# Expert rows of a two-part transformer kernel: first-table rows of both token tiles ahead of second-table rows, other shares of rows per stage, and the second layer's modulation moved to the first block's scores

## The reference, cut to what matters

```python
for l in range(DEPTH):
    mod   = (silu(c)     @ w_mod[l] + b_mod[l])     # six rows of 1024: shift, scale, gate, twice
    mod_c = (silu(c_ctx) @ w_mod[l] + b_mod[l])     # the same for the context
    ...                                              # mixer: attention, pooling, convolution, gates, w_out
    xn2 = modulate(rms_norm(h, norm2_g[l]), mod[:, 3], mod[:, 4])
    h = h + mod[:, 5] * peer_ffn(xn2, ...)           # and for the context where not last

def peer_ffn(x, w_q, sub_keys, u_emb, v_emb):        # per chunk of 128 tokens
    q = (xc @ w_q) ...                               # 8 heads, two halves of 128
    ... top 16 of each half's 128 keys, top 16 of the 256 sums -> eidx, gate = softmax
    u = u_emb[eidx]                                  # 128 rows of 1024 for each token
    hid = gelu(einsum('td,thkd->thk', xc, u))
    return einsum('thk,thkd->td', gate * hid, v_emb[eidx])
```

## Time and profile before

| | |
|---|---|
| median of 3 runs | 3910.57 us (3910.49 to 3939.74) |
| the profiled execution | 3915.19 us, span of its instructions 3913.4 us |
| DVE busy | 2804.7 us (72%) |
| PE busy | 1916.9 us (49%), weight loads 1225.8 us |
| POOL busy | 1842.7 us (47%) |
| ACT busy | 402.6 us (10%) |
| DMA | 1111.66 MB, mean 284 GB/s; gathers 811.71 MB of it |

### The profile page before, as it was taken

How to read it: one execution, slowest core, us unless ns; L and a number is a source line. 1 busy time by engine, 2 the same in 40 slices (tenths; PEclk the granted TensorE clock), 3 DMA queues, 4 the chain that set the end, 5 groups by cost and what they waited for, 6 DMA issues and landing times.

```text
span 3913.4 us, 27165 instructions
## 1 busy us (share of the span) xinstructions
PE 1916.9 (49%) x8842; PEld 1225.8 (31%) x8842; DVE 2804.7 (72%) x4787; ACT 402.6 (10%) x917; POOL 1842.7 (47%) x1556
## 2 busy tenths in 40 slices
PE   6899993076885698883206000019899800000000
PEld 3558482044532346463202000004475700000000
DVE  2321279945869987759997999975411699998998
ACT  1310110023211310010001000002300100000000
POOL 0000033423636766627746777740000377577776
PEclk8999997588786699996557555559999955555555
DMA  6754487767889899969969999963144588699999
GB/s 206 248 178 166 161 289 254 222 232 258 293 313 349 302 355 372 391 243 402 392 232 358 372 380 396 374 249 140 66 149 167 198 291 283 235 377 361 386 377 345
DMA packets 402292, 1111.66 MB, mean 284 GB/s; under 512 B 37121, under 2 KB 91585, under 8 KB 401378
## 3 DMA queue, kind: packets, MB, share of 16 engines
q0 software_dynamic: 223024, 811.71, 56.2%
q1 hardware_dynamic: 179128, 298.22, 21.6%
HBM read 1105.52 MB, written 4.29 MB: 284 GB/s over the span
## 4 chain that ended last, share of the span: by engine, by line
DVE 36%; PE 33%; POOL 13%; DMA 8%; issue 8%; ACT 2%; DVEq 0%; SPq 0%; ACTq 0%; POOLq 0%
PE PS L419 30%; POOL ring L975 13%; DVE acc L1332 12%; DVE ring L1326 11%; DMA ring<-in_peer_u,eidx 3%; DMA wring<-in_w_in 2%; DVE work L1774 1%; DVE work L1777 1%; DVE work L1386 1%; DVE work L1775 1%; ACT work L1002 1%; DMA ring<-in_peer_v,eidx 1%; DVE work L1389 1%; DVE work L1833 1%; DVE work L1836 1%
## 5 line engine op out<-in xcount | busy, mean ns | idle before, releaser
L975 POOL DMA_INDIRECT ring<-in_peer_u,eidx x768 | 940.2, 1224 | 1297.8 <-DVE eidx L1839 515.7
L975 POOL DMA_INDIRECT ring<-in_peer_v,eidx x768 | 892.4, 1162 | 615.4 <-DVE acc L1332 219.6
L1332 DVE SCALAR_TENSOR_TENSOR acc<-ring,small,acc 128x1024 f32<-128x1024 f32 x762 | 977.4, 1283 | 90.9 <-DMA ring<-in_peer_v,eidx 27.9
L1326 DVE SCALAR_TENSOR_TENSOR ring<-ring,xn_peer 128x1024 f32<-128x1024 f32 x768 | 932.9, 1218 | 77.6 <-DMA ring<-in_peer_u,eidx 67.5
L419 PE MATMUL PS<-wring,xnT 128*128 128x512 f32 (+2 forms) x1728 | 738.9, 589 | 17.8 <-issue 13.1
L419 PE MATMUL PS<-xnT,wring 128*128 128x128 f32 (+1 forms) x2896 | 484.1, 330 | 28.1 <-DMA wring<-in_w_in 17.2
L419 PEld LDWEIGHTS PS<-xnT,wring 128*128 128x128 f32 x2896 | 440.6, 195 | 70.9 <-DMA wring<-in_w_in 19.6
L419 PEld LDWEIGHTS PS<-wring,xnT 128*128 128x128 f32 x1728 | 330.2, 194 | 418.9 <-issue 411.2
L427 PE MATMUL PS<-const,work 128*128 128x128 f32 (+1 forms) x358 | 59.2, 331 | 696.8 <-DVE work L1389 676.8
L1002 ACT ACTIVATE work<-PS 128x512 f32<-128x512 f32 (+5 forms) x377 | 189.2, 525 | 1133.7 <-PE PS L419 771.8
L419 PE MATMUL PS<-wring,work 128*128 128x512 f32 (+2 forms) x640 | 265.1, 576 | 29.1 <-DMA wring<-in_w_out 17.3
(11 more groups left out here) (163 smaller groups left out, 1486.0 us busy)
## 6 DMA issues: line engine op xcount, KB each, us to landing
wring<-in_w_in SPq DMA_DIRECT2D x128, 1024.0 KB, 7.4
wring<-in_w_mod SPq DMA_DIRECT2D x48, 1024.0 KB, 12.9
wring<-in_peer_wq SPq DMA_DIRECT2D x24, 1024.0 KB, 7.3
wring<-in_ab_w_in SPq DMA_DIRECT2D x13, 1024.0 KB, 21.9
wring<-in_conv_out_w SPq DMA_DIRECT2D x12, 1024.0 KB, 5.1
wring<-in_w_out SPq DMA_DIRECT2D x12, 1024.0 KB, 9.3
ring<-in_peer_u,eidx POOLq DMA_INDIRECT x768, 6.4
ring<-in_peer_v,eidx POOLq DMA_INDIRECT x768, 6.1
```

The costliest lines, as they stand in the source:

```text
L975: pool.indirect_dma_start(ring[:, m % NG, :], None, table, bass.IndirectOffsetOnAxis(ap=eidx[:, r % 2, t, k:k + 1], axis=0))\
L1326: v.scalar_tensor_tensor(out=slot, in0=slot, scalar=1.0, in1=xn_peer[:, t, :], op0=ALU.mult, op1=ALU.mult, accum_out=hid[:, k:k + 1]).then ...
L1332: v.scalar_tensor_tensor(out=acc[:, :], in0=slot, scalar=wgt[:, k - NSEL:k - NSEL + 1], in1=acc[:, :], op0=ALU.mult, op1=ALU.add).then_inc ...
```

## The change

The order of items within a run becomes: first-table rows of tile 0, of tile 1, then second-table rows and gate row of tile 0, of tile 1. For that, `hid` and `wgt` get a copy for each tile. Tile 0 of run 0 is turned at "ab", ahead of the first scores, and tile 1 at "gated c", between the z gates and y of the latent attention. `PACE` and `PER_PRODUCT` are lower in "ab" and "c"; in mixer 1 the pace is lower and the number per product goes from 5 to 8. In `gelu_first` fewer rows than before may be left; four rows are done between it and `gelu_last` in runs 1 and 2.

The second layer's modulation moves from behind run 1's queries to the place between `vb` and the first scores: on PE, on ACT (ahead of `top_exps(0)`), in SP's order of weights (ahead of the z weights of ab_in). Its bias comes in one DMA of 12 rows instead of three, into a space that is free there; the matmul that adds it takes a column of the identity and 12 rows instead of ones and one row. `mod_out` for it stands before block ("ab_in", 9), and DVE waits for `mod_stored` before it first writes `O_TOK`, which shares its space.

```diff
-PACE = {"front0": 0.3, "ab": 0.8, "c": 0.8, "m1": 0.7, "front1": 0.5, "m3": 0.8, "front2": 0.5}
-PER_PRODUCT = {"ab": 6, "c": 6, "m1": 5, "m3": 4}
+PACE = {"front0": 0.3, "ab": 0.5, "c": 0.5, "m1": 0.5, "front1": 0.5, "m3": 0.8, "front2": 0.5}
+PER_PRODUCT = {"ab": 4, "c": 4, "m1": 8, "m3": 4}
-TURN_AT = {"c": (0, 0), "pooled 1": (0, 1)}
+TURN_AT = {"ab": (0, 0), "gated c": (0, 1)}
 # weight_blocks
-    halves("ab_in", "ab_w_in", 0, 7 * WB, 3328, 7)
+    halves("ab_in", "ab_w_in", 0, 7 * WB, 9 * WB, 7)
+    halves("mod1_0", "w_mod", 1, 0, 2 * D)
+    halves("mod1_1", "w_mod", 1, 2 * D, 6 * D)
+    halves("ab_in", "ab_w_in", 0, 9 * WB, 3328, 9)
...
-    halves("mod1_0", "w_mod", 1, 0, 2 * D)
-    halves("mod1_1", "w_mod", 1, 2 * D, 6 * D)
 # items
+        RUN_ITEMS = T * (2 * NSEL + 1)
+        def u_item(r, t, k):
+            return RUN_NO[r] * RUN_ITEMS + t * NSEL + k
+        def v_item(r, t, k):
+            return RUN_NO[r] * RUN_ITEMS + T * NSEL + t * (NSEL + 1) + k
 # PE, modulation
-                    pe.wait_ge(modb_landed, 48 * (l + 1))
+                    pe.wait_ge(modb_landed, 16 * (l + 1))
...
-                        ins = pe.matmul(strips[j], const[0:1, C_ONES:C_POOL], MODROW[l][m // 4][0:1, at_b:at_b + P], start=False, stop=True)
+                        ins = pe.matmul(strips[j], this, MODB[l][:, j * P:(j + 1) * P], start=False, stop=True)
 # PE, first_block
                 tokens("ab_in", 2, xnT, ("vb",), 7)
+                modulation(1, 0)
+                modulation(1, 1)
 # SP
-                    sp.wait_ge(*at("product", "wo", 1, T - 1, 1))
-                for n in range(3):
-                    sp.dma_start(MODROW[l][n][0:1, :], ...).then_inc(modb_landed, 16)
+                    sp.wait_ge(*at("product", "sub", 0, T - 1, GROUPS - 1))
+                sp.dma_start(MODB[l], DR["b_mod_2"][l].rearrange("(m c) -> m c", m=12)).then_inc(modb_landed, 16)
...
-                ("ab_in", 9): [(load_bias, 2), (load_bias, 3)],
+                ("ab_in", 9): [(mod_out, 1, 0, 3), (load_bias, 2), (load_bias, 3)],
-                ("k3", 0): [(mod_out, 1, 0, 3), (load_rows, "sc_3", "sh_3"), (load_smalls, 1)],
+                ("k3", 0): [(load_rows, "sc_3", "sh_3"), (load_smalls, 1)],
 # POOL
             for r in range(3):
                 for t in range(T):
+                    rows_in(r, t, DR["peer_u_2"].rearrange("l e d -> (l e) d"), u_item)
+                for t in range(T):
+                    rows_in(r, t, DR["peer_v_2"].rearrange("l e d -> (l e) d"), v_item)
 # ACT, first_block
                 same("act", "vb_ready")
+                modulation(1, 0)
+                modulation(1, 1)
                 top_exps(0)
+                turn("ab")
 # DVE
-                    if m >= min(rows_at["chosen"], rows_at["weighted"] * NI + NSEL):
+                    if m >= rows_at["chosen"] if u_row else r * T + t >= rows_at["weighted"]:
                         return
...
+                        if s == "ab" and u == 2:
+                            v.wait_ge(mod_stored, 128)
...
+                turn_to_v("ab")
                 pace("ab")
...
-            expert_rows(2 * NI * T)
             gelu_first(1, 0)
+            expert_rows(4)
             gelu_last(1, 0)
             pace("m3")
             mixer(3, [("product", "xnT", ("m", 1), T - 1, 1)])
-            expert_rows(NI * T)
             gelu_first(1, 1)
+            expert_rows(4)
             gelu_last(1, 1)
-            expert_rows(NI * T)
+            expert_rows(RUN_ITEMS)
...
             for t in range(T):
-                expert_rows(NI * T)
                 gelu_first(2, t)
+                expert_rows(4)
                 gelu_last(2, t)
-            expert_rows(NI * T)
+            expert_rows(RUN_ITEMS)
```

More of the change, by code:

```diff
@@ L290, in program @@
         early = ring[:, :, :].rearrange("p n d -> p (n d)")
-        MODROW = [[early[0:2, b:b + 2 * D] for b in (0, 2048, 4096)], [work[0:2, b:b + 2 * D] for b in (0, 2048, 4096)]]
+        MODB = [early[0:12, 0:512], work[0:12, 11776:12288]]
         mod_rows = xn_peer[:, :, :].rearrange("p t d -> p (t d)")
         MODT = [[mod_rows[:, 512 * a:512 * b].rearrange("p (a b) -> p a b", b=P) for a, b in ((0, 1), (1, 3))],
-                [wk(6144, 4, P), wk(6656, 8, P)]]
+                [wk(10240, 4, P), wk(10752, 8, P)]]
         hot = early[0:33, 6144:7168].rearrange("p (g j) -> p g j", g=2)
@@ L965, in _, with rows_in @@
             pool.wait_ge(mod_stored, 64)
-            def rows_in(r, t, table, kinds):
+            def rows_in(r, t, table, item):
                 for k in range(NSEL):
-                    m = item(r, t, kinds * NSEL + k)
-                    if not kinds and k % (NSEL // GROUPS) == 0:
+                    m = item(r, t, k)
+                    if item is u_item and k % (NSEL // GROUPS) == 0:
                         pool.wait_ge(*at("experts", r, t, k // (NSEL // GROUPS)))
@@ L1013, in gelu_exp @@
                 act.wait_ge(*at("gelu_arg", r, t))
-                A(act.activation(wgt, wgt, ACT.Exp, scale=-1.0), "gelu_exp", r, t)
+                A(act.activation(wgt[:, t, :], wgt[:, t, :], ACT.Exp, scale=-1.0), "gelu_exp", r, t)
             def root(dst, src, waits, *tag):
@@ L1294, in _ @@
             peer_front(1)
-            modulation(1, 0)
-            modulation(1, 1)
             top_exps(1)
@@ L1317, in expert_rows @@
                     m = rows_at["next"]
[L1318 removed]
+                    r, j = m // RUN_ITEMS, m % RUN_ITEMS
+                    u_row = j < T * NSEL
+                    t, k = (j // NSEL, j % NSEL) if u_row else ((j - T * NSEL) // (NSEL + 1), (j - T * NSEL) % (NSEL + 1))
+                    if m >= rows_at["chosen"] if u_row else r * T + t >= rows_at["weighted"]:
                         return
                     rows_at["next"] += 1
[L1321 removed]
                     slot = ring[:, m % NG, :]
                     v.wait_ge(g_landed[m % NG], 16 * (m // NG + 1))
[L1324 removed]
+                    if u_row:
                         v.scalar_tensor_tensor(out=slot, in0=slot, scalar=1.0, in1=xn_peer[:, t, :], op0=ALU.mult,
[L1327 to L1330 removed]
+                                               op1=ALU.mult, accum_out=hid[:, t, k:k + 1]).then_inc(slot_used, 1)
+                    elif k == 0:
+                        v.tensor_scalar(acc[:, :], slot, wgt[:, t, 0:1], None, ALU.mult).then_inc(slot_used, 1)
+                    elif k < NSEL:
                         v.wait_ge(slot_used, m)
[L1332 removed]
+                        v.scalar_tensor_tensor(out=acc[:, :], in0=slot, scalar=wgt[:, t, k:k + 1], in1=acc[:, :],
                                                op0=ALU.mult, op1=ALU.add).then_inc(slot_used, 1)
@@ L1783, in mixed_norm @@
                 v.wait_ge(*row_wait(f"m2_{r}"))
+                assert rows_at["next"] >= (v_item(r - 1, 0, 0) if r else 0)
                 for t in range(T):
@@ L1839, in choose @@
                 D_(v.tensor_copy(eidx[:, r % 2, t, at_n], placef[:, 0, at_n]), "experts", r, t, g)
-                rows_at["chosen"] = job * NI + n * (g + 1) if g < GROUPS - 1 else (job + 1) * NI
+                rows_at["chosen"] = u_item(r, t, n * (g + 1))
             def peer_front(r, free, beside_first=None):
```

47 lines of the change are left out of this document (17 added, 30 removed).

## The result

The changed kernel takes 3944.66 us (median of 20 runs, 3933.88 to 3953.37), the kernel before on the same chip 3918.55 (20 runs, 3901.42 to 3947.79): **1.0059** times as long [1.0045, 1.0074] (a ratio over all runs; the quotient of the two medians is 1.0067). The forecast was 13 us less than before, in a range up to 3938; measured is some 0.3 to 0.6% more. The profiled span went from 3913.4 to 3944.1, so 30.7 us have to be found.

What follows compares the result with a forecast made beforehand. The prediction took VectorE (DVE), nearly always busy with gathered rows, as the bound. Its stage terms summed to -13 us, giving 3902 us for an execution like the profiled one and 3898 for the median, range 3855 to 3938.

Steps and rivals of the forecast that it cites:

- the flush at the gates of "c": Latent attention's gates: 38 rows at 1.32 = 50 us; with GELU, ten rows and additions 71 against 35 now, +36.
- "ab", with the modulation beside front0: First attention: flush of 30 rows 40 us, GELU 3.8, 8 fewer rows -10, modulation beside front0 3; together +37.
- "c" up to the gates: Latent attention before its gates: 10, 11 and 6 fewer rows give -20 us, -12 if the chain holds.
- mixer 1: heads, attention, behind it: Mixer 1: ten more rows in the heads +4 us, 67 rows become 48 in the attention -17, behind it -3.
- front1: Choosing of run 1: -12 and -12 us, then two full blocks of 42.5 and 5 closing rows +35; together +11.
- run 3's keys, rows before mixer 2: 5 more rows beside run 3's keys and values +3 us; before mixer 2, 68 first-table rows out, 29 second-table in, -50.
- front2: Choosing of run 2: two full choose blocks and 5 rows more, +35 us.
- the end: Last stretch of rows alone: 34 first-table rows fewer at 1.44 us each, -49 us.
- The modulation: Second modulation beside front0: matmuls free, weights in near 742, no DVE wait near 762; 3 us charged there, 12 returned in front1.
- (1): Rival: bytes decide in mixer 1, chains do not bind; part behind its attention gains 24 us, total 3859; chance 0.28.
- (2): Rival: modulation weights end at 791, so DVE stalls 29 us at 762; total 3927; chance 0.09.
- (3): Rival: crowded rows cost +20 us in mixer 1, +9 at the gates of "c", whose chain gives only 12; 3938; chance 0.08.

Runs made afterwards that it cites:

- m1_rates_old: Changed kernel with mixer 1's rates as before (0.7 and 5), those of "ab" and "c" as changed; ratio 1.0034 to the kernel before.
- after_again: The changed kernel unchanged, measured a second time with the kernel before beside it; ratio 1.0029.
- mod_back: Changed kernel with the second modulation put back behind run 1's queries; ratio 1.0057 to the kernel before.
- first_rates_old: Changed kernel with the rates of "ab" and "c" as before (0.8 and 6), mixer 1's as changed; ratio 0.9927 to the kernel before.
- turn_late: Changed kernel, its rates kept, with tile 1 of run 0 turned at mixer 1's pooling instead of "gated c"; ratio 0.9955 to the kernel before.
- ab_rates_old: Changed kernel with the rates of "ab" alone as before (0.8 and 6); ratio 0.9944 to the kernel before.
- c_rates_old: Changed kernel with the rates of "c" alone as before (0.8 and 6); ratio 0.9992 to the kernel before.
- ab_more: Changed kernel with all rates as before, except 10 instead of 6 rows per product in "ab"; ratio 0.9980 to the kernel before.
- before_again: The kernel before, unchanged, profiled once more; one run, 3921.45 us.
- mod_only: Kernel before with the second modulation alone moved, old order and old rates; ratio 0.9965 to the kernel before.
- fronts_07: Changed kernel with all rates as before, and pace 0.7 in place of 0.5 in front1 and front2; ratio 0.9946 to the kernel before.

## Why the prediction was wrong

The sign was wrong, and the range missed by 7 us. Of the 47 us between 3898 and 3944.66, 8 are not the change's: the kernel before has 3910.57 in its three runs and 3918.55 in twenty. The counts and the places where things wait were forecast rightly. What failed is what rows cost in the places they were moved to, and most of all one term of the sum, the flush at the gates of "c". In the forecast's terms, with the closing steps of front1 and front2 counted to them as there:

| step | forecast | measured |
|---|---|---|
| "ab", with the modulation beside front0 | +37 | +39 |
| "c" up to the gates, and flush with y | -20, +36 | -14, +48 |
| mixer 1: heads, attention, behind it | +4, -17, -3 | +13, -18, 0 |
| front1 | +11 | +13 |
| run 3's keys, rows before mixer 2 | +3, -50 | +3, -43 |
| mixer 2 | 0 | +2 |
| front2 | +35 | +33 |
| the end | -49 | -45 |

The sum of the right column is +31, of the left one -13.

- **The flush at the gates, the step that failed most.** It was priced "38 rows at 1.32 = 50", the price of a row that has the DMA engines to itself. It took 62.5 us, 1.64 a row (62 to 63 us in all four traces that have it), because the weights of the coming products come at just that place (a third of the engines' time) and PE has nothing to do beside it once y is done at 1121. The forecast named this ("c_out's weights and the next ones want the DMA engines, too") and gave it at most 9 us, and the rival that the crowding costs 9. The flush in "ab" took 45.5 us for 30 rows, 1.52 each, not 40; no weights came beside that one (from 764 to 811 the DMA share was 0.87, all of it gathers), so its price has another reason, which stays open.
- **"c" up to the gates.** 27 rows fewer give 14 us, 0.5 each, as by the chain's bound (-12), not 20.
- **The heads.** +13, not +4. The ten further rows were thought to be half hidden behind the wait for q. But the last two places of 8, 16 rows in 22.1 us, stand between the operands and the first score's reduction. In m1_rates_old, with 9 rows fewer there, the heads take 144.9 us for after_again's 156.9: 1.33 a row, nothing hidden.
- **Rows alone.** The -90 for 68 first-table rows held. But "a row alone costs another price in the new order", named as what would make the forecast wrong, happened: the 60 that remain, items 710 to 769, took 92.4 us from first start to last, 1.57 each, where the same rows took 1.29 before (+16). They now lie directly behind run 3's keys, where the last weights for mixer 2 still come; the first 31 took 1.67 each, the last 30 took 1.46. The place is dear in the old order too: its second-table items there, 671 to 769, took 1.46 each, not the 1.39 of a second-table row alone, and with them gone some 7 us came back. At the end the 34 rows were priced at 1.44; that was misread from the earlier trace rows. The first 8 us of the window from 3540 hold four second-table rows, the gate row and the addition to the stream, so 160 us is not the time of 111 first-table rows. From start to start that tile's rows took 175.5 us for 127, 1.38 each. 34 of them are 47, and the 94 that stay cost 1.42 now for 1.37, +5.
- **A window cut too early.** The 131.9 us of mixer 1's attention with 67 rows begin 6.7 us before its first score's reduction at 1242.7. Cut there it takes 125.8 us, which makes a row 0.95 us and not 1.03; after, the attention takes 107.1 with 48 rows. The step came out near enough all the same (-17 and -18).
- **Right.** The count of rows everywhere. The modulation: last matmuls at 755 (forecast 742), no wait of DVE near 762, front0 as long as before, choose blocks of 41.5 to 42.5 in front1. The part of mixer 1 behind the attention: 0 against -3, which was the step held to be the least certain. By the Trainium skill's figure (DMA: Bandwidth & Descriptors, section Where 436 GB/s comes from) of about 358 GB/s, the forecast's estimate of the modulation's end was 788; the trace has 755, so it does not bear that figure out here, where one core ran alone. The engines moved 386 GB/s between 611 and 755 and 406 in the flush at the gates.
- **The rivals.** (1), bytes decide and chains don't: refuted, as the part behind the attention did not gain. (2), a late modulation: refuted, DVE has no wait for ACT near 762, and mod_back leaves "ab" and "c" as they are; but the room was 7 us and not 20. (3), the crowding costs: half right. Its price at the gates (+9) and its -12 in "c" are near what was seen; its +20 from 8 per product in mixer 1 is not, as m1_rates_old shows them to be neutral there. It got a chance of 0.08.
- **What the forecast did not ask.** It charged the flush and credited the lower rates as two separate terms. Beside each other they read: 35 rows taken out of "ab" and "c" for 30 us, put back at the gates for 50 or more. That the lower rates lose could be seen from the forecast's own terms, before any run. Restored, they bring 1.0029 to 0.9927.

**What is shown and what is not.** Shown, each by an edit of its own: the changed kernel loses by the low rates of "ab" and "c" together with the early turn of tile 1. The rates restored remove the loss with the turn in place (first_rates_old against after_again, same group: 1.0029 to 0.9927), and the turn restored removes it with the low rates in place (turn_late, 0.9955). What joins the two is the flush: ab_rates_old (0.9944) and c_rates_old (0.9992) shrink it to 13 and 10 rows. Their ratios come from a group without the changed kernel, and c_rates_old's 0.4% is hardly more than the 0.3% by which groups can differ; but its stages show the same, with 4 rows more in "c" in 17 us less. Mixer 1's rates are neutral over the whole mixer. The modulation's move is worth 0.35% in the old order and 0.43 to 0.46% in the new one with old rates. In the changed kernel itself it could not be determined: front1 is 13 us shorter with the move, but the ratios are 1.0057 without it against 1.0059 and 1.0029 with it, none of them measured side by side. Not shown is how the miss of the sum divides between the flush (+12), the heads (+9), the rows before mixer 2 (+7) and the rest, beyond single traces. Open is also why the changed kernel stands at 1.0059 in one measurement and 1.0029 in the other, and why ab_more's ratio is worse than its stages.

## What to carry to other kernels

Work that fills gaps has a marginal price at each place, and it rises as the place fills: from 0.5 us a row in "ab" to 1.0, from 1.04 in a choose block to 1.42. So compare the last unit taken out of one place with what the same unit costs where it ends up, not the averages. A phase change that must be complete (a flush) turns whatever the earlier places left undone into a stall of the whole chain, and there it competes with weights that were prefetched for what comes next; either do enough before it, or put the change where no product waits.

## What the hardware showed that was not expected

First-table rows alone, bound by the DMA engines (share 0.96 to 1.03), do not have one price. Take the same 60 rows, the last of run 1's second tile: from start to start they took 1.29, 1.30 and 1.42 us each in the three traces of the old order (before, before_again, mod_only) and 1.47 to 1.57 in the thirteen traces of the new order that do them behind run 3's keys (all but fronts_07). A part of that is the place, beside mixer 2's last weights. The rest is not explained: with no weights beside them, the gathers moved 396 GB/s at a share of 1.01 in before (2270 to 2400) and 360 at 0.98 in after (2230 to 2291). Second-table rows, where a tile of them is done alone, keep 1.39 to 1.41 us nearly always, DVE's own pace, which mostly hides such variation; but one tile of mod_back, two of first_rates_old and one of fronts_07 took 1.45 to 1.47. No run here tells why the gathers vary. And a row's landing goes from 6.1 us to 11.3 where 1 MB weight blocks share the engines, while the engines' total, 406 GB/s, is higher there than in any other stage of that trace's table above.
